# Ten value slots and a new order of the loads in a decoder step with cached attention

## The chip, the core and the metric

The kernel runs on one core of a Trainium2 chip. The metric is the device time of one execution in microseconds (us), of which the median of several executions counts.

## The reference, cut to what matters

One layer of a decoder works on 512 prompt tokens and on 8 sample sequences of 8 new tokens each (64 tokens). All of it is 32-bit floating point.

```
proj = x @ w_in                       # (576 tokens, 1024) @ (1024, 4096)
q, k, v, g_att, b, c, h, g_conv = split(proj, 8)      # 512 wide each
att = dilated_attention(q, [cache_k; k], [cache_v; v]) * silu(g_att)
z   = b * conv3(c * h) * silu(g_conv)
y   = layer_norm(alpha * x + [att, z] @ w_out)
```

Attention has 8 heads of 64. The prompt attends to itself; each sample also attends to a cache of 2,048 past positions, of which the three windows (128 by 1, 512 by 4, 2048 by 16) touch 1,280. The outputs hold y, the new keys and values, the convolution state, and the whole cache copied and moved on by 8 positions.

## The kernel before, in words

**Tiles and rounds.** The input projection is cut into 32 weight tiles of 1024 x 128 (512 KB each). Three come first, then four rounds (i = 0 to 3), one for each pair of heads, with first tile t0 = 3 + 8i. A round projects c (C), h (H), b (B), the convolution's gate (G_CONV), the next round's values (V), the attention's gate, and the next round's q and k; the last round has five tiles. Each product is made in three passes over a high and a low part of both factors (`product`, L993 to L999), in two halves of 288 tokens, into the PSUM banks `pj_a` and `pj_b`. Between the halves TensorE works on the round's attention: scores, transposes and values of the prompt, scores against the cached keys (four pieces, `sample_scores`, L1084), and products with the cached values (ten pieces, `sample_values`, L1125), spread over the round's last three tiles. After the rounds comes the output projection over `wo`, with the layer norm behind it.

**A weight tile's way.** `load_w` (L227, on SyncE's queue) fills one of two slots of `w_raw`; it waits until the low part of the tile two before is made. `split_hi` on ScalarE (L396) rounds it to `w_hi`, waiting for the load and for TensorE to be done with that slot; `split_lo` on VectorE (L678) makes `w_lo`; then `project` (L1001) may run.

**Cached keys and values.** `load_k(i, c)` (L234) fills one of four slots of `k_buf` (1,280 KB), `load_v(i, n)` (L241) one of `V_SLOTS` = 8 slots of `v_buf` (512 KB), piece n of round i in slot (10i + n) mod 8. A load waits until the piece that lay in its slot is used. All loads are issued in program order by SyncE (L249 to L356), a wait holds up all behind it, and they form one DMA queue. The order by hand is in L282 to L303: in steps j = 0 to 4 of round i a weight tile and then a key piece of round i+1 (in round 0 two value pieces too), then two more weight tiles, values 8 and 9 of round i, `save_v` (the prompt's values out), values 0 and 1 of round i+1, a weight tile, values 2 to 7, `save_k`. Then the eight tiles of `wo` (L307) go into the room of `k_buf` and its neighbours, each as its room comes free, and last values 8 and 9 of round 3 (L328).

**Copies of the cache.** 60 DMAs from HBM to HBM copy the cache's parts to the outputs (24 of the unused part, 16 of keys with 1,280 KB, 20 of values; 1,024 KB each but the keys'). ScalarE issues them with `copy_next` (L434) between its other work, on its own queue: 5 before the rounds, 12 in each of rounds 0 to 2, 10 in the last, the rest behind it. The end of the kernel waits for all of them (L358).

**ScalarE and VectorE** each run a list written by hand (`act_round` L556, `act_last_round` L605, `dve_round` L853, `dve_last_round` L894). In the last round the splits of `wo` (`split_wo` L538, `split_wo_lo` L794) lie between the exponentials of the gates (`exp_gate` L502) and the pieces of the gates (`gate_half` L759). `gate_half` makes 1 + exp, its reciprocal, the product with `zb` (the convolution's result, from `conv_out_half` L824) or with `o_pr`, and the product with the bank of the gate's projection (L777), which frees that bank for the next `project`. `out_sample` (L527) copies the sample's attention from the bank `sc` to `o_s`; `sample_out_turn` (L1149) transposes it in the next round. `y_pad` holds the convolution's sums (`conv_taps`, L780).

Of the kernel before, what the change touches and what calls it, by code (L numbers as in the profile page):

```python
# [7 lines left out]
P = 128  # L8
# [36 lines left out]
V_SLOTS = 8  # L45
# [26 lines left out]
def layer_step(nc, d):  # L72

    with ExitStack() as ctx:
# [16 lines left out]
        zb = sb("zb", [P, NT])  # L91
# [26 lines left out]
        o_s = sb("o_s", [P, 2 * P], stack=early)  # L118
# [46 lines left out]
        g_exp, g_step = sem("g_exp"), sem("g_step")  # L165
# [7 lines left out]
        v_stage = gcs  # L173

# [51 lines left out]
        def _(sp):  # L226
# [55 lines left out]
            for i in range(NPAIR - 1):  # L282
                t0 = tile0(i)
                for j in range(5):
                    load_w(t0 + 3 + j)
                    if j:
                        load_k(i + 1, j - 1)
                    if i == 0 and j < 4:
                        load_v(0, 2 * j)
                        load_v(0, 2 * j + 1)  # L290
                load_w(t0 + 8)
                load_w(t0 + 9)
                load_v(i, 8)
                load_v(i, 9)
                save_v(i + 1)
                load_v(i + 1, 0)
                load_v(i + 1, 1)
                load_w(t0 + 10)
                for n in range(2, 8):
                    load_v(i + 1, n)  # L300
                save_k(i + 1)
            load_w(W_TILES - 2)
            load_w(W_TILES - 1)  # L303

# [8 lines left out]
            load_wo(0)  # L313
            sp.wait_ge(k_used, pieces + 2)
            load_wo(1)
            sp.wait_ge(k_used, pieces + 3)
            load_wo(2)
            sp.wait_ge(k_used, pieces + 4)
# [9 lines left out]
            load_v(NPAIR - 1, 8)  # L328
            load_v(NPAIR - 1, 9)
# [65 lines left out]
        def _(act):  # L395
# [86 lines left out]
            copy_next()  # L482
# [73 lines left out]
            def act_round(i):  # L556
# [10 lines left out]
                copy_next()  # L567
# [37 lines left out]
            def act_last_round(i):  # L605
# [23 lines left out]
                split_wo(1)  # L629
                out_prompt(i)  # L630
# [8 lines left out]
                split_wo(4)  # L639
                split_wo(5)  # L640
# [9 lines left out]
                copy_next()  # L650
                for t in TOKEN_TILES[1:]:
                    if t == QT:
                        out_sample_turned(i)
                        split_sample()
                    else:
# [21 lines left out]
        def _(dve):  # L677
# [81 lines left out]
            def gate_half(i, gate, h):  # L759
# [9 lines left out]
                if gate == 0:  # L769
                    nc.vector.tensor_tensor(rg[:, c], rg[:, c], zb[:, c], ALU.mult).then_inc(g_step, 1)  # L770
# [9 lines left out]
            def conv_taps(i, tap):  # L780
                n = PAD_COLS - 2
                cw = conv_w[:, i * CONV_WIDTH + tap:i * CONV_WIDTH + tap + 1]
                if tap == 0:
# [3 lines left out]
                    dve.wait_ge(padded, i + 1)  # L787
                    nc.vector.tensor_scalar(y_pad[:, 0:n], u_pad[:, 0:n], cw, None, ALU.mult).then_inc(y_step, 1)
# [625 lines left out]
```

## Time and profile before

| | us |
|---|---|
| median of 3 executions | 382.79 (381.42 to 383.18) |
| the profiled execution, its own time | 379.59 |
| its span, first to last instruction | 377.5 |
| TensorE busy (PE) | 353.8 |
| VectorE, ScalarE busy | 198.5, 117.4 |
| DMA moved | 141.06 MB, mean 374 GB/s |

The profile is of one execution. PE is TensorE's matmuls, PEld its weight loads, DVE is VectorE, ACT ScalarE, POOL GpSimd; SPq and ACTq are the issues of DMAs by SyncE and ScalarE. Times are us from the first instruction. A wait is named by the instruction that waited and by what ended its wait. Matmul records count from issue to their modelled end, so a busy PE says that it is fed, not that it is at its peak.

### The profile page before, as it was taken

To read this page: it belongs to the slowest core of one execution; us is meant where nothing else is said; L and a number is where in the kernel's file an instruction comes from. 1 tells how busy PE (TensorE), PEld (TensorE's weight loads), DVE (VectorE), ACT (ScalarE), POOL (GpSimd) and SP (SyncE) were. 2 spreads that over 40 slices of the span, in tenths; PEclk is the share of its full clock that TensorE was granted. 3 is DMA by queue.
4 is the path that set the end of the run, shared out by engine and by line. 5 is a ranking of instruction groups with operands and counts; after the bars stand their busy time and mean duration, and the time that the engine had idled before them with its cause. 6 is when DMAs were issued, how large, how long until landed. Compare 5 with 4: busy or idle time off the path is not lost.

```text
span 377.5 us, 7664 instructions
## 1 busy us (share of the span) xinstructions
PE 353.8 (94%) x3256; PEld 311.3 (82%) x3256; DVE 198.5 (53%) x371; ACT 117.4 (31%) x236; POOL 10.9 (3%) x28
## 2 busy tenths in 40 slices
PE   1999999997999999999999799999998998999991
PEld 1899888896988888999988689999787997888780
DVE  2533446817314368571242486711536799284765
ACT  4523423313213243431241243412525643220100
POOL 0010000000000000001000000010000002000000
PEclk9999999998999999999999999999999999999997
DMA  7999999999999999899999999999999886999931
GB/s 279 408 413 423 419 417 423 419 423 422 413 416 418 421 379 413 316 403 369 394 418 418 383 418 395 423 394 406 415 416 408 326 333 216 366 317 366 361 124 56
DMA packets 34547, 141.06 MB, mean 374 GB/s; under 512 B 3409, under 2 KB 3793, under 8 KB 32465
## 3 DMA queue, kind: packets, MB, share of 16 engines
q1 hardware_dynamic: 18194, 73.46, 48.9%
q10 hardware_dynamic: 16320, 67.11, 45.8%
q8 instruction: 26, 0.43, 0.4%
q14 instruction: 7, 0.06, 0.0%
HBM read 135.80 MB, written 71.86 MB: 550 GB/s over the span
## 4 chain that ended last, share of the span: by engine, by line
PE 62%; DMA 28%; DVE 4%; ACT 2%; SPq 2%; issue 1%; ACTq 0%
DMA w_raw<-in_w_tiles 26%; PE pj_a L997 7%; PE pj_b L997 6%; PE pj_a L999 6%; PE pj_a L998 6%; PE pj_b L998 6%; PE pj_b L999 6%; PE sc L1136 5%; PE px L1294 3%; PE px L1296 3%; PE px L1295 3%; PE sc L1100 2%; DVE w_lo L681 2%; ACT w_hi L402 2%; DMA k_buf<-in_xT 2%; PE po L1079 1%
## 5 line engine op out<-in xcount | busy, mean ns | idle before, releaser
L997 PE MATMUL pj_a<-x_hi,w_hi 128*128 128x288 f32 x256 | 79.8, 312 | 9.7 <-DVE x_lo L688 8.3
L997 PE MATMUL pj_b<-x_hi,w_hi 128*128 128x288 f32 x256 | 79.1, 309 | 0.0
L998 PE MATMUL pj_a<-x_lo,w_hi 128*128 128x288 f32 x256 | 76.5, 299 | 0.0
L999 PE MATMUL pj_a<-x_hi,w_lo 128*128 128x288 f32 x256 | 76.5, 299 | 0.0
L998 PE MATMUL pj_b<-x_lo,w_hi 128*128 128x288 f32 x256 | 76.1, 297 | 0.0
L999 PE MATMUL pj_b<-x_hi,w_lo 128*128 128x288 f32 x256 | 75.9, 297 | 0.0
L681 DVE TENSOR_TENSOR w_lo<-w_raw,w_hi 128x1024 fp32r<-128x1024 f32 x32 | 39.1, 1223 | 50.9 <-ACT w_hi L402 50.9
L997 PEld LDWEIGHTS pj_a<-x_hi,w_hi 128*128 128x128 f32 x256 | 49.2, 192 | 18.3 <-issue 9.3
L402 ACT CAST w_hi<-w_raw 128x1024 fp32r<-128x1024 f32 x32 | 33.5, 1046 | 87.3 <-DMA w_raw<-in_w_tiles 55.6
L997 PEld LDWEIGHTS pj_b<-x_hi,w_hi 128*128 128x128 f32 x256 | 48.6, 190 | 4.1 <-issue 2.6
L998 PEld LDWEIGHTS pj_a<-x_lo,w_hi 128*128 128x128 f32 x256 | 49.3, 193 | 0.0
L999 PEld LDWEIGHTS pj_a<-x_hi,w_lo 128*128 128x128 f32 x256 | 49.2, 192 | 0.0
L998 PEld LDWEIGHTS pj_b<-x_lo,w_hi 128*128 128x128 f32 x256 | 48.6, 190 | 0.0
L999 PEld LDWEIGHTS pj_b<-x_hi,w_lo 128*128 128x128 f32 x256 | 48.5, 190 | 0.0
L767 DVE RECIPROCAL rg<-rg 128x288 f32<-128x288 f32 x16 | 31.2, 1953 | 0.6
L488 ACT ACTIVATE p_pr<-p_pr,stat 128x512 f32<-128x512 f32 (+3 forms) x32 | 17.7, 555 | 27.1 <-DVE stat L732 27.1
L732 DVE CUSTOM_DVE_ANT_0 p_pr<-px,mask_pr 128x512 f32<-128x512 f32 (+3 forms) x32 | 14.4, 486 | 18.8 <-PE px L1049 18.8
L1136 PE MATMUL sc<-v_buf,pt_s 128*32 128x128 f32 x640 | 21.4, 276 | 0.0
L1100 PE MATMUL sc<-k_buf,q_bd 128*32 128x320 f32 x256 | 20.5, 438 | 0.9 <-DVE stat L754 0.9
L1294 PE MATMUL px<-wo,x_hi 128*128 128x512 f32 x48 | 19.1, 397 | 1.2 <-issue 1.2
L1296 PE MATMUL px<-wo,x_lo 128*128 128x512 f32 x48 | 19.0, 396 | 0.0
L1136 PEld LDWEIGHTS sc<-v_buf,pt_s 128*32 128x32 f32 x640 | 16.3, 109 | 3.3 <-issue 3.0
(124 smaller groups left out, 403.4 us busy)
## 6 DMA issues: line engine op xcount, KB each, us to landing
k_buf<-in_k_used SPq DMA_DIRECT2D x16, 1280.0 KB, 15.2
v_buf<-in_v_used SPq DMA_DIRECT2D x40, 512.0 KB, 18.4
out_k_used_out<-in_k_used ACTq DMA_DIRECT2D x16, 1280.0 KB, 11.6
out_v_used_out<-in_v_used ACTq DMA_DIRECT2D x20, 1024.0 KB, 10.8
w_raw<-in_w_tiles SPq DMA_DIRECT2D x32, 512.0 KB, 11.5
out_k_rest_out<-in_k_rest ACTq DMA_DIRECT2D x12, 1024.0 KB, 11.5
out_v_rest_out<-in_v_rest ACTq DMA_DIRECT2D x12, 1024.0 KB, 11.3
wo_raw<-in_w_out SPq DMA_DIRECT2D x8, 512.0 KB, 8.6
```

Of the source, the lines that this page charges most:

```text
L402: nc.scalar.copy(w_hi[:, c], w_raw[:, c]).then_inc(w_hi_done, 1)
L488: nc.scalar.activation(p, p, ACT.Exp, bias=negmax_pr[:, e:e + 1], scale=-1.0, accum_out=sum_pr[:, e:e + 1]).then_inc(pr_exp, 1)
L681: nc.vector.tensor_tensor(w_lo[:, c], w_raw[:, c], w_hi[:, c].bitcast(F32), ALU.subtract)\
L732: nc.vector.tensor_tensor_reduce(out=p_pr[:, e * SEQ:e * SEQ + w], in0=px[e][:, 0:w], in1=mask_pr[:, SEQ - w:], scale=-SCALE, scalar=BIG, ...
L767: nc.vector.reciprocal(rg[:, c], rg[:, c]).then_inc(g_step, 1)
L997: nc.tensor.matmul(out, w_hi[:, w], x_hi[:, c], start=(k == 0), stop=False)
L998: nc.tensor.matmul(out, w_hi[:, w], x_lo[:, c], start=False, stop=False)
L999: return nc.tensor.matmul(out, w_lo[:, w], x_hi[:, c], start=False, stop=(k == KT - 1))
L1100: last = nc.tensor.matmul(sc[r * 32:r * 32 + 32, 0:K_COLS], q, k_buf[:, k0:k0 + K_COLS], start=(b == 0), stop=(b == 1 and not ends), skip_ ...
L1136: last = nc.tensor.matmul(sc[r * 32:r * 32 + 32, b * P:(b + 1) * P], pt_s[:, t * P + r * 32:t * P + r * 32 + 32], v_buf[:, v0:v0 + P], sta ...
L1294: nc.tensor.matmul(out, x_hi[:, tok], wo[:, hi], start=(n == 0), stop=False)
L1296: last = nc.tensor.matmul(out, x_lo[:, tok], wo[:, hi], start=False, stop=(n == KT - 1))
```

## The change

Four things. `v_buf` has ten slots instead of eight, one for each piece of a round. Room for them comes from two buffers that go: z is written over the convolution's sums in `y_pad` instead of to `zb`, and the sample's attention `o_s` lies in the first 256 columns of `y_pad`. The gate's product with z is for the second half two instructions (224 and 64 columns) instead of one, and the first convolution tap waits in rounds 1 to 3 for the transposes of `o_s`. SyncE's order is new: each of the steps j = 0 to 4 loads a weight tile and then values 2j and 2j+1 of the same round, keys of the next round follow (three at the round's end, the fourth in the next step 0), and in the last round the values are loaded between the last weight tiles and the first tiles of `wo`. Four of ScalarE's cache copies go later: one from before the rounds and one from each of rounds 0 to 2; two of them are issued in the last round, one at its end and one in the output projection.

```diff
--- before.py
+++ after.py
@@ -42,7 +42,7 @@
 K_COLS = USED // K_PIECES
 K_SLOT = DEC_BATCH * K_COLS
 V_PIECES = 10
-V_SLOTS = 8
+V_SLOTS = V_PIECES
 QT = SEQ // P
 X_CHUNKS = ((0, 1), (1, 3), (3, 5), (5, 7), (7, 8))
 PAD_COLS = 2 + SEQ + DEC_BATCH * (2 + DEC_SEQ)
@@ -88,7 +88,6 @@
         w_lo = sb("w_lo", [P, 2 * 1024], F32R)
         mix = sb("mix", [P, 2 * NHP * NT])
         gcs = sb("gcs", [P, NT])
-        zb = sb("zb", [P, NT])
         rg = sb("rg", [P, NT])
         u_pad = sb("u_pad", [P, PAD_COLS])
         y_pad = sb("y_pad", [P, PAD_COLS])
@@ -115,7 +114,6 @@
         v_new = sb("v_new", [NS, 2 * P], stack=early)
         pt_s = sb("pt_s", [P, (USED_TILES + 1) * P], stack=early)
         v_buf = sb("v_buf", [P, V_SLOTS * 1024], stack=early)
-        o_s = sb("o_s", [P, 2 * P], stack=early)
         o_pr = sb("o_pr", [P, SEQ], stack=early)
         early.close()
         as_loaded = ctx.enter_context(ExitStack())
@@ -162,7 +160,7 @@
             sem("s_masked"), sem("s_max"), sem("s_exp"), sem("s_inv"), sem("s_norm"))
         s_turned, s_moved, s_pv, s_out = sem("s_turned"), sem("s_moved"), sem("s_pv"), sem("s_out")
         so_turned, so_moved, s_mixed = sem("so_turned"), sem("so_moved"), sem("s_mixed")
-        g_exp, g_step = sem("g_exp"), sem("g_step")
+        g_exp, g_step, g_prompt = sem("g_exp"), sem("g_step"), sem("g_prompt")
         m_hi_done, m_lo_done, wo_hi_done, wo_lo_done = (
             sem("m_hi_done"), sem("m_lo_done"), sem("wo_hi_done"), sem("wo_lo_done"))
         low_read, r_high = sem("low_read"), sem("r_high")
@@ -171,6 +169,8 @@
 
         x_raw = k_buf[:, 0:KT * NT]
         v_stage = gcs
+
+        o_s = y_pad[:, 0:2 * P]
 
 
         xs = w_hi[:, 0:KT * P].rearrange("p (k two t) -> p k two t", two=2, t=NS)
@@ -280,27 +280,30 @@
             load_k(0, 3)
             save_k(0)
             for i in range(NPAIR - 1):
+
+
                 t0 = tile0(i)
                 for j in range(5):
                     load_w(t0 + 3 + j)
-                    if j:
-                        load_k(i + 1, j - 1)
-                    if i == 0 and j < 4:
-                        load_v(0, 2 * j)
-                        load_v(0, 2 * j + 1)
+                    if i and j == 0:
+                        load_k(i, 3)
+                    load_v(i, 2 * j)
+                    load_v(i, 2 * j + 1)
                 load_w(t0 + 8)
+                load_k(i + 1, 0)
                 load_w(t0 + 9)
-                load_v(i, 8)
-                load_v(i, 9)
                 save_v(i + 1)
-                load_v(i + 1, 0)
-                load_v(i + 1, 1)
+                load_k(i + 1, 1)
                 load_w(t0 + 10)
-                for n in range(2, 8):
-                    load_v(i + 1, n)
+                load_k(i + 1, 2)
                 save_k(i + 1)
             load_w(W_TILES - 2)
+            load_k(NPAIR - 1, 3)
+            load_v(NPAIR - 1, 0)
+            load_v(NPAIR - 1, 1)
             load_w(W_TILES - 1)
+            load_v(NPAIR - 1, 2)
+            load_v(NPAIR - 1, 3)
 
 
 
@@ -311,10 +314,16 @@
             pieces = K_PIECES * (NPAIR - 1)
             sp.wait_ge(k_used, pieces + 1)
             load_wo(0)
+            load_v(NPAIR - 1, 4)
+            load_v(NPAIR - 1, 5)
             sp.wait_ge(k_used, pieces + 2)
             load_wo(1)
+            load_v(NPAIR - 1, 6)
+            load_v(NPAIR - 1, 7)
             sp.wait_ge(k_used, pieces + 3)
             load_wo(2)
+            load_v(NPAIR - 1, 8)
+            load_v(NPAIR - 1, 9)
             sp.wait_ge(k_used, pieces + 4)
             load_wo(3)
             load_wo(4)
@@ -325,8 +334,6 @@
             load_wo(6)
             sp.wait_ge(s_masked, K_PIECES * NPAIR)
             load_wo(7)
-            load_v(NPAIR - 1, 8)
-            load_v(NPAIR - 1, 9)
 
 
             sp.wait_ge(s_pv, NPAIR)
@@ -479,7 +486,6 @@
             copy_next()
             copy_kk(0)
             split_hi(4)
-            copy_next()
 
             def exp_prompt(i, u):
                 for e in range(2):
@@ -564,7 +570,6 @@
                 split_hi(t0 + 2)
                 copy_next()
                 move_prompt(i, 0)
-                copy_next()
                 exp_prompt(i, 1)
                 split_hi(t0 + 3)
                 move_prompt(i, 1)
@@ -627,6 +632,7 @@
                 split_hi(t0 + 4)
                 copy_next()
                 split_wo(1)
+                copy_next()
                 out_prompt(i)
                 move_sample(i, 0)
                 move_sample(i, 1)
@@ -637,6 +643,7 @@
                 split_wo(3)
                 exp_gate(t0 + G_CONV, 1)
                 split_wo(4)
+                copy_next()
                 split_wo(5)
                 exp_gate(gate_tile(i), 0)
                 copy_next()
@@ -648,10 +655,12 @@
                 out_sample(i)
                 copy_next()
                 copy_next()
+                copy_next()
                 for t in TOKEN_TILES[1:]:
                     if t == QT:
                         out_sample_turned(i)
                         split_sample()
+                        copy_next()
                     else:
                         split_mix(1 + t)
                         copy_next()
@@ -766,8 +775,14 @@
                 dve.wait_ge(g_step, step + 1)
                 nc.vector.reciprocal(rg[:, c], rg[:, c]).then_inc(g_step, 1)
                 dve.wait_ge(g_step, step + 2)
-                if gate == 0:
-                    nc.vector.tensor_tensor(rg[:, c], rg[:, c], zb[:, c], ALU.mult).then_inc(g_step, 1)
+                if gate == 0 and h == 0:
+                    nc.vector.tensor_tensor(rg[:, c], rg[:, c], y_pad[:, c], ALU.mult).then_inc(g_step, 1)
+                elif gate == 0:
+                    nc.vector.tensor_tensor(rg[:, HALF:SEQ], rg[:, HALF:SEQ], y_pad[:, HALF:SEQ], ALU.mult)\
+                        .then_inc(g_prompt, 1)
+                    r = rg[:, SEQ:].rearrange("p (b t) -> p b t", t=DEC_SEQ)
+                    nc.vector.tensor_tensor(r, r, y_s[:, :, 0:DEC_SEQ], ALU.mult).then_inc(g_step, 1)
+                    dve.wait_ge(g_prompt, i + 1)
                 else:
                     dve.wait_ge(pr_out, i + 1)
                     e = slice(h * HALF, min((h + 1) * HALF, SEQ))
@@ -785,6 +800,9 @@
                     dve.wait_ge(pj_read[0], tile0(i) + 2)
                     dve.wait_ge(pj_read[1], tile0(i) + 2)
                     dve.wait_ge(padded, i + 1)
+                    if i:
+
+                        dve.wait_ge(so_turned, i)
                     nc.vector.tensor_scalar(y_pad[:, 0:n], u_pad[:, 0:n], cw, None, ALU.mult).then_inc(y_step, 1)
                 else:
                     dve.wait_ge(y_step, 2 * i + tap)
@@ -826,12 +844,12 @@
                 dve.wait_ge(y_done, i + 1)
                 dve.wait_ge(pj_done[h], tile0(i) + B + 1)
                 if h == 0:
-                    nc.vector.tensor_tensor(zb[:, 0:HALF], pj[0][:, 0:HALF], y_pad[:, 0:HALF], ALU.mult)\
+                    nc.vector.tensor_tensor(y_pad[:, 0:HALF], pj[0][:, 0:HALF], y_pad[:, 0:HALF], ALU.mult)\
                         .then_inc(pj_read[0], 1)
                 else:
-                    nc.vector.tensor_tensor(zb[:, HALF:SEQ], pj[1][:, 0:HP_LEFT], y_pad[:, HALF:SEQ], ALU.mult)\
+                    nc.vector.tensor_tensor(y_pad[:, HALF:SEQ], pj[1][:, 0:HP_LEFT], y_pad[:, HALF:SEQ], ALU.mult)\
                         .then_inc(z_done, 1)
-                    nc.vector.tensor_tensor(zb[:, SEQ:].rearrange("p (b t) -> p b t", t=DEC_SEQ),
+                    nc.vector.tensor_tensor(y_s[:, :, 0:DEC_SEQ],
                                             pj[1][:, HP_LEFT:HALF].rearrange("p (b t) -> p b t", t=DEC_SEQ),
                                             y_s[:, :, 0:DEC_SEQ], ALU.mult).then_inc(pj_read[1], 1)
```

## Rows read from the trace of the kernel before

**Rows 1.** The page: PE's busy time, TensorE's clock and DMA in 40 slices of 9.4 us.
```profile
PE 353.8 (94%) x3256; PEld 311.3 (82%) x3256; DVE 198.5 (53%) x371; ACT 117.4 (31%) x236; POOL 10.9 (3%) x28
...
PEclk9999999998999999999999999999999999999997
DMA  7999999999999999899999999999999886999931
```
**Rows 2.** Waits of PE, whole span: line waited for: us in total, times, longest.
```profile
PE pj_a L997 <- DVE x_lo L688: 8.3, 2, 7.2
PE po L1079 <- ACT pt_pr L494: 3.0, 3, 1.3
PE pj_a L997 <- DVE mix L777: 1.2, 1, 1.2
PE px L1294 <- issue: 1.2, 1, 1.2
PE sc L1100 <- DVE stat L754: 0.9, 1, 0.9
PE pt L1120 <- ACT pt_s L515: 0.9, 1, 0.9
```
**Rows 3.** Chain of waits, 83 to 92 us: start us, us, what.
```profile
63.14 20.74 DMA w_raw<-in_w_tiles
...
89.55 0.58 PE pj_a L997
```
**Rows 4.** Busy by stretch: PE, PEld, DVE, ACT, POOL, clock, DMA share, GB/s.
```profile
89.00:92.00 3.00, 2.45 (x10) 2.48 (x11) 2.93 (x5) 0.00 (x0) 0.00 (x0) 0.56 1.02 425
92.00:96.00 4.00, 4.00 (x53) 3.64 (x52) 1.91 (x3) 1.77 (x4) 0.00 (x0) 0.91 1.01 419
```
**Rows 5.** Timeline, 208 to 216 us.
```profile
210.99 1.05 ACT L402 CAST w_hi<-w_raw 128x1024 fp32r<-128x1024 f32 x1 [11.18 <-DMA w_raw<-in_w_tiles]
...
212.84 0.88 PE L1079 MATMUL po<-pt_pr,v_rows 128*64 128x128 f32 x12 [1.31 <-ACT pt_pr L494]
...
214.59 1.28 PE L1100 MATMUL sc<-k_buf,q_bd 128*32 128x320 f32 x16 [0.87 <-DVE stat L754]
```
**Rows 6.** Timeline of SyncE's issues, 245 to 302 us.
```profile
245.86 2.12 SPq L246 DMA_DIRECT2D v_buf<-in_v_used  x2
```
**Rows 7.** Landing of the two v_buf loads issued in 246 to 248 us.
```profile
DMA to landing us min/median/max: 9.0/10.3/11.6
```
**Rows 8.** Timeline of PE, 257.5 to 259.5 us.
```profile
258.44 1.08 PE L1136 MATMUL sc<-v_buf,pt_s 128*32 128x128 f32 x32
```
**Rows 9.** Landing of the weight tile issued in 245 to 246 us.
```profile
DMA to landing us min/median/max: 6.4/6.4/6.4
```
**Rows 10.** DMA by queue, 252 to 262 us (q1 SyncE's, q10 ScalarE's): packets, MB, share.
```profile
q1 hardware_dynamic: 590, 1.61, 41.4%
```
**Rows 11.** DMA by queue, 262 to 290 us.
```profile
q1 hardware_dynamic: 1994, 7.01, 61.8%
q10 hardware_dynamic: 1180, 4.54, 40.2%
```
**Rows 12.** Timeline of ScalarE, 255 to 330 us.
```profile
298.43 1.07 ACT L540 CAST wo<-wo_raw 128x1024 fp32r<-128x1024 f32 x1
...
300.55 1.05 ACT L540 CAST wo<-wo_raw 128x1024 fp32r<-128x1024 f32 x1
```
**Rows 13.** Timeline of VectorE, 300 to 309 us.
```profile
303.00 0.46 DVE L770 TENSOR_TENSOR rg<-rg,zb 128x288 f32<-128x288 f32 x1
303.49 0.46 DVE L777 TENSOR_TENSOR mix<-pj_a,rg 128x288 f32<-128x288 f32 x1
```
**Rows 14.** Chain of waits, 296 to 322 us.
```profile
305.30 0.33 PE pj_a L997
...
309.67 0.33 PE pj_b L997
```
**Rows 15.** DMA issues, 316 to 362 us.
```profile
out_v_used_out<-in_v_used ACTq DMA_DIRECT2D x11, 1024.0 KB, 16.8
```

## The prediction

> **What bounds the kernel now.** The page first: PE is busy 353.8 us of 377.5, and the slices show it fed from the second to the last; the DMA engines are just as full until about 290 us [rows 1]. So two resources lie close together, and the waits must say which one decides. PE's waits name 15.5 us in all. Of these 8.3 us are the start (x must land) and 1.2 us the step to the output projection; what is left inside is 6.0 us in a few places [rows 2]. TensorE therefore sets the time, and the loads set it only where they are late enough to stop it.
>
> Two places are made by late loads. The first is at 86 to 89.5 us. The chain shows a weight tile issued at 63.14 that landed after 20.74 us; behind it ScalarE and VectorE, which work in a fixed order, did the gate late, and PE began its next tile at 89.55 [rows 3]. PE lost 0.85 us (L1120) and 1.23 us (L777), rounded in the view [rows 2]. Right after it the granted clock of 89 to 92 us is 0.56 of full speed and of 92 to 96 us 0.91 [rows 4]: TensorE fell from 2.4 to 1.2 GHz for a time, which cost 3 x 0.44 + 4 x 0.09 = 1.7 us more. The second is at 211: ScalarE waited 11.18 us for a weight tile until 210.99, and PE lost 1.31 and 0.87 us [rows 5]. Both times the tile stood in SyncE's queue behind key and value pieces.
>
> One edge costs nothing in this profile, but is thin. Value piece 9 of round 2 is the second of two issued from 245.86 on (so at about 246.5), and takes 11.6 us [rows 6, 7]: it lands at 258.1. PE starts on pieces 8 and 9 at 258.44, 1.08 us for both [rows 8], so it needs piece 9 at 258.9: 0.8 us to spare. The edge is in every one of rounds 0 to 2, since the piece waits for a slot. The profiled execution took 379.59 us and the median 382.79, 3.2 us more; this edge is where I would look for them, but no row shows it.
>
> **The change, part by part.** *Ten slots and the new order, rounds 0 to 2.* Before, a round's last eight value loads came as a burst at its end, with one weight tile behind six of them, and in steps 1 to 3 of round 0 each carried a weight tile, a key piece and two value pieces (0.52 + 1.31 + 1.05 = 2.9 MB). Now a step is a tile and two values, 1.6 MB, and the keys come behind. The tile that took 20.74 us loses two key pieces ahead of it, 2.6 MB, and one copy beside it. At SyncE's rate of 7.01 MB in 28 us, 0.25 MB/us [rows 11], that is 10 us earlier, and 2.1 us would give PE its wait back. The tile of 211 had the round's ten value issues (5.2 MB) put ahead of it from 169 us on, now two key pieces (2.6 MB): again 2.6 MB or 10 us, where 2.2 us are enough. I take both stalls and the slow clock as gone: 0.85 + 1.23 + 1.7 + 1.31 + 0.87 = 6.0 us gained. Bounds: 2.2 us (only one goes) to 7 us (the 0.67 and 1.05 us at L1079 in the last round shrink too; they come from the order of ScalarE's list, so I expect them to stay). No wait on a slot is new: a value piece now waits for the same piece of the round before, which is long used. Keys are issued 25 us and more ahead of use.
>
> *Values 8 and 9* now come with step 4, some 25 us before use, so the thin edge goes. I count half of the 3.2 us, 1.6 us, for the median and nothing for the profiled execution; bounds 0 and 3.2.
>
> *The last round pays.* Ten values and a key piece are now loaded there, where two values were. Count what SyncE's queue must move after 252 us, when the weight tile issued at 245.49 has landed in 6.4 us, so the queue is nearly empty [rows 9]. Until `wo` tile 2 these are, in order: outputs 0.30, key 1.31, tile 0.52, key 1.31, output 0.30, tile 0.52, key 1.31, values 0 and 1 1.05, tile 0.52, values 2 and 3 1.05, wo0 0.52, values 4 and 5 1.05, wo1 0.52, values 6 and 7 1.05, wo2 0.52: 11.9 MB. Before, the queue moved 1.61 MB from 252 to 262 and 7.01 MB from 262 to 290 [rows 10, 11], 8.6 MB by 290. So wo2 lacks 3.2 MB, at 0.25 MB/us 13.0 us: it lands at 303.0. ScalarE took it at 298.43 [rows 12]: `split_wo(2)` stands 4.6 us longer, and behind it on ScalarE the gate's exponential. The chain from there ended with the gate's product at 303.49 + 0.46 = 303.95, which frees the bank; PE began that tile only at 305.30 [rows 13, 14], so 1.35 us are covered, and 3.2 us reach PE. wo3 lies 1.57 MB behind, 309.3 instead of the 300.55 of its split [rows 12]. Its two splits take 1.05 and 1.2 us, the next gate half 3.3 us (the chain of rows 13 once more), to 314.9; PE comes there at 309.67 + 3.2 = 312.9 [rows 14]: 2.0 us more. Debt 5.2 us. Wo4 to wo7 (2.1 MB, 8.4 us, to 317.7) are needed for the output projection, which would start at 322: covered.
>
> The rate is the unknown. At the full 0.41 MB/us of both queues together [rows 11] wo2 lands at 298 and the debt is 0. At the 0.16 MB/us of 252 to 262 [rows 10] it lands at 310 and the debt passes 10 us. I take 0.25, since ScalarE's copies there are issued as in 262 to 290. Two things I set off against each other: four copies there are of 1,280 KB instead of 1,024 (+1.05 MB), and one copy less waits in the queue at 252.
>
> *Copies.* Before 252 us four are gone, a relief for the rounds that is in the gain already. Eleven were issued after 316 us [rows 15], now 13, 2.1 MB more. The DMA slices fall to 3 and 1 tenths only in the last 19 us [rows 1], and 2.1 MB at the page's 374 GB/s is 5.6 us: hidden. Cover gone, it would be those 5.6 us.
>
> *z in `y_pad`, `o_s` in `y_pad`.* One product of 0.46 us [rows 13] becomes two, at most 0.46 us more in each of four rounds, hidden by the 1.35 us above and by VectorE's own waits. The new wait of the first tap is for transposes that PE does two tiles earlier; VectorE's list stands behind it, but it ends before. Nothing.
>
> **Sum.** -6.0 + 5.2 = -0.8 us for the profiled execution, 378.8; for the median 382.8 - 0.8 - 1.6 = 380.4 us.
>
> **The rivals.** *No debt (B).* ScalarE's copies are issued from its list, so once it stands at a split no copy follows and SyncE's queue gets nearly everything. For it: at 290 to 310 the DMA slices were below full [rows 1]. Then 382.8 - 6.0 - 1.6 = 375.2 us. Against it: two or three copies are already queued when the wait begins.
>
> *A larger debt (C), the slower side.* While both queues have work they share evenly, 0.205 MB/us each (half of 0.41). wo2 then lands at 290 + 3.24/0.205 = 305.8, 6.1 us reach PE; wo3 at 313.5, its gate half ends at 319.1, PE comes at 315.7: 3.4 us more. Debt 9.5 us, 382.8 - 6.0 + 9.5 = 386.3 us (the saved edge comes back as another one in the last round). It decides from 0.22 MB/us down. For it: in 252 to 262 SyncE's queue had only 1.61 MB in 10 us [rows 10]. Against it: 7.01 to 4.54 MB in the 28 us behind [rows 11]. The Trainium skill (DMA: Bandwidth & Descriptors, Queues, rings and completion order) says that each DMA engine takes turns between the queue rows for which it has work; by that rule C holds wherever a copy is pending, and the 7.01 to 4.54 would only mean that at times none was.
>
> *It does not do what it says (D).* The median's waits come from something else than the loads, and gain and debt cancel: 382.8 us.
>
> **How the numbers follow.** A measurement of this kernel tells a change from none from about 0.5% on, 1.9 us: faster is below 380.9, slower above 384.7. The forecast case (debt 3.5 to 6.5 us, 378.7 to 381.7) has 0.41, of which 0.27 faster and 0.14 same. B 0.16, all faster. C 0.27, all slower. D 0.16: 0.01 faster, 0.11 same, 0.04 slower. Together faster 0.44, same 0.25, slower 0.31. The range takes in B's edge and C: 375.0 to 387.0. The likeliest case's own range is 378.7 to 381.7 us.
>
> **What would show it.** Right: no wait of PE of over 0.5 us between 80 and 230 us, no fall of the clock there, weight tiles landing in 6 to 14 us, value 9 tens of us before use; then ScalarE waiting at L540 for wo2 and wo3, and PE waiting before the two halves of the last gate's tile. B would show those splits without a wait. C would show 6 us before the first half. The forecast is wrong if PE waits for keys in rounds 1 to 3, if the last copy lands after the last y, or if the early waits stay where they are though the loads land early.

## The result, and the profile after

The change makes the kernel slower by 1%: 387.06 us median of 13 executions (384.54 to 390.07) against 383.18 us (380.18 to 384.91), ratio 1.0102 with a 95% interval of 1.0075 to 1.0129. The forecast was 380.4 us, faster; the range ended at 387.0, and the rival with the larger debt stood at 386.3. A single profiled execution can lie off its median: the one of before took 379.59 us, 3.6 us below its median, the one after 385.67 us, 1.4 us below. So differences between the two traces overstate the loss of the medians (3.9 us) by some 2 us.

The page of the profile after, the lines that answer to [rows 1], and PE's waits over the whole span, which answer to [rows 2]:

```profile
PE 356.8 (93%) x3256; PEld 314.2 (82%) x3256; DVE 200.0 (52%) x375; ACT 118.0 (31%) x236; POOL 11.9 (3%) x28
...
PEclk9999999999999999999999999999996969999998
DMA  7999999599999995999999989999999996999991
```
```profile
PE pj_a L1015 <- DVE x_lo L697: 8.5, 2, 7.4
PE po L1097 <- ACT pt_pr L500: 6.9, 3, 5.3
PE pj_a L1015 <- DVE mix L792: 2.6, 1, 2.6
PE px L1312 <- issue: 0.8, 1, 0.8
PE pj_a L1015 <- ACT gcs L459: 0.2, 1, 0.2
```

The DMA slices now have three dips before 235 us (the two 5s and the 8): the rounds have DMA time to spare. PE has no wait between the start (the first 20 us) and 265 us; the two early stalls and the slow clock there are gone. The gain shows at the first tile of the last round. The timeline of PE has it in the kernel before, and then in the one after, at:

```profile
260.02 0.40 PE L997 MATMUL pj_a<-x_hi,w_hi 128*128 128x288 f32 x1
```
```profile
254.41 0.40 PE L1015 MATMUL pj_a<-x_hi,w_hi 128*128 128x288 f32 x1
```

That is 5.6 us earlier, where 6.0 were forecast. From there on it is lost and more. ScalarE's timeline after, at the splits of the `wo` tiles (start, duration, and in brackets what it waited for), answers to [rows 12]:

```profile
291.72 1.04 ACT L546 CAST wo<-wo_raw 128x1024 fp32r<-128x1024 f32 x1 [10.67 <-DMA wo_raw<-in_w_out]
292.67 1.41 ACT L515 ACTIVATE p_s<-p_s,stat 128x1344 f32<-128x1344 f32 x1
...
294.08 0.41 ACT L500 COPY pt_pr<-pt 128x128 f32<-128x128 f32 x2
...
303.76 1.05 ACT L546 CAST wo<-wo_raw 128x1024 fp32r<-128x1024 f32 x1 [5.16 <-DMA wo_raw<-in_w_out]
...
309.10 1.05 ACT L546 CAST wo<-wo_raw 128x1024 fp32r<-128x1024 f32 x1 [3.57 <-DMA wo_raw<-in_w_out]
```

And PE's timeline, the two waits that follow from these:

```profile
294.54 0.69 PE L1097 MATMUL po<-pt_pr,v_rows 128*64 128x128 f32 x4 [5.33 <-ACT pt_pr L500]
```
```profile
309.41 0.58 PE L1015 MATMUL pj_a<-x_hi,w_hi 128*128 128x288 f32 x1 [2.60 <-DVE mix L792]
```

Read them as one chain. ScalarE stood at `split_wo(0)` for 10.67 us until wo0 landed; the sample's exponential and the move of the prompt's last probabilities (L500) are behind it in its list; PE waited 5.33 us for that move. The same tile that PE began at 305.30 before [rows 14] begins at 309.41. PE's last matmul, in the kernel before and in the one after:

```profile
369.02 0.40 PE L1296 MATMUL px<-wo,x_lo 128*128 128x512 f32 x1
```
```profile
375.46 0.40 PE L1314 MATMUL px<-wo,x_lo 128*128 128x512 f32 x1
```

It ends at 375.9 instead of 369.4. From the first tile of the last round to that end it was 109.4 us and is 121.5: a debt of 12 us between these two traces, against 5.2 forecast. 7.4 us are more waiting (10.3 us instead of 2.9 from 262 us on), and most of the rest is the slow clock around the waits, in the busy time by stretch (the last three numbers are the clock as a share of 2.4 GHz, the DMA share and GB/s):

```profile
289.00:295.00 6.00, 0.67 (x6) 0.29 (x4) 1.98 (x3) 3.28 (x6) 0.00 (x0) 0.72 1.03 421
295.00:300.00 5.00, 4.85 (x30) 4.62 (x27) 4.22 (x7) 2.94 (x5) 0.00 (x0) 0.65 1.02 419
307.00:316.00 9.00, 6.59 (x44) 6.35 (x48) 7.84 (x11) 3.86 (x5) 0.00 (x0) 0.62 1.00 394
```

The last views are the two queues, the one of 262 to 290 us answering to [rows 11] (q1 SyncE's, q10 ScalarE's: packets, MB, share):

```profile
q1 hardware_dynamic: 1431, 5.89, 51.3%
q10 hardware_dynamic: 1284, 5.77, 50.0%
```

SyncE's queue moved 5.89 MB instead of 7.01. These were the theories when the experiments began: V, what SyncE's queue has to bring in the last round fixes when the `wo` tiles land; with the rivals O (their place behind the values), C (the copies moved there), K (the clock) and L (the in-order lists, which pass a wait for `wo` on to TensorE).

### The profile page after: what moved, and what is told of

It is laid out like the page before. It is cut to its first block, busy times and chain, and to the rows that moved or that the text cites. A ratio compares the mean times of both kernels' runs of the same rounds, so it can differ in the third digit from the quotient of the medians.

```text
span 383.9 us, 7672 instructions
## 1 busy us (share of the span) xinstructions
PE 356.8 (93%) x3256; PEld 314.2 (82%) x3256; DVE 200.0 (52%) x375; ACT 118.0 (31%) x236; POOL 11.9 (3%) x28
## 4 chain that ended last, share of the span: by engine, by line
PE 83%; DMA 8%; SPq 3%; DVE 3%; ACT 1%; issue 1%; ACTq 0%; DVEq 0%
PE pj_a L1015 10%; PE pj_b L1015 9%; PE pj_a L1016 8%; PE pj_a L1017 8%; PE pj_b L1017 8%; PE pj_b L1016 8%; DMA wo_raw<-in_w_out 6%; PE sc L1154 5%; PE sc L1118 4%; PE px L1312 3%; PE px L1314 3%; PE px L1313 3%; PE px L1067 3%; PE po L1097 2%; SPq L246 2%; PE pt L1084 2%
## 5 line engine op out<-in xcount | busy, mean ns | idle before, releaser
L1015 PE MATMUL pj_a<-x_hi,w_hi 128*128 128x288 f32 x256 | 80.9, 316 | 11.3 <-DVE x_lo L697 8.5
L1016 PE MATMUL pj_a<-x_lo,w_hi 128*128 128x288 f32 x256 | 77.4, 302 | 0.0
L1017 PE MATMUL pj_a<-x_hi,w_lo 128*128 128x288 f32 x256 | 77.3, 302 | 0.0
L1015 PEld LDWEIGHTS pj_a<-x_hi,w_hi 128*128 128x128 f32 x256 | 50.1, 196 | 19.9 <-issue 10.7
L1016 PEld LDWEIGHTS pj_a<-x_lo,w_hi 128*128 128x128 f32 x256 | 50.2, 196 | 0.0
L1017 PEld LDWEIGHTS pj_a<-x_hi,w_lo 128*128 128x128 f32 x256 | 50.1, 196 | 0.0
L500 ACT COPY pt_pr<-pt 128x512 f32<-128x512 f32 (+3 forms) x32 | 12.0, 429 | 28.0 <-PE pt L1084 28.0
## 6 DMA issues: line engine op xcount, KB each, us to landing
out_k_rest_out<-in_k_rest ACTq DMA_DIRECT2D x12, 1024.0 KB, 10.7
```

The source lines that it names most:

```text
L500: nc.scalar.copy(pt_pr[:, e * SEQ:e * SEQ + width(u)], pt[e][:, 0:width(u)]).then_inc(pr_moved, 1)
L1015: nc.tensor.matmul(out, w_hi[:, w], x_hi[:, c], start=(k == 0), stop=False)
L1016: nc.tensor.matmul(out, w_hi[:, w], x_lo[:, c], start=False, stop=False)
L1017: return nc.tensor.matmul(out, w_lo[:, w], x_hi[:, c], start=False, stop=(k == KT - 1))
```

## The experiments

All ratios are to the kernel before, run on the same chip; that kernel's median was 380.9 to 381.0 us in them. "Last matmul" and landings are of the one profiled execution of each.

### Fewer bytes in the last round

```diff
# SyncE, on the changed kernel (cut)
                     load_w(t0 + 3 + j)
+                    if i == 2 and 1 <= j <= 3:
+                        load_k(3, j - 1)
...
+                load_k(3, 3)                       # round 2, with tile t0 + 8
+                for n in range(4): load_v(3, n)    # behind tile t0 + 10
```


> The changed kernel, but in round 2 the keys of round 3 are loaded as before the change (one piece in each of steps 1 to 3, the fourth behind), and values 0 to 3 of round 3 come behind the last weight tiles of round 2: 3.9 MB of keys and 1.0 MB of values leave the last round's queue. Theory V (volume: what SyncE's queue must bring in the last round fixes when the wo tiles land, and the early gain is lost against it): wo0 lands before 284 us instead of 291.7, wo2 before 295 instead of 303.7, the PE waits of 5.3 and 2.6 us go below 1 us each, both slow-clock stretches of the last round go; the last matmul 10 to 12 us earlier, ratio to the kernel before 0.975 to 0.985. Rival O (order: it is only that values stand ahead of wo): less than 3 us better, ratio 1.00 to 1.01. Rival C (the two copies moved into the last round): unchanged, 1.01.

Measured: 380.54 us, ratio 1.0007 (0.9981 to 1.0032). wo0 was split at 286.3 and wo2 at 295.7 us, 5.5 and 8.0 us earlier. ScalarE's wait for wo0 shrank from 10.7 to 3.7 us and no longer reached PE, but then ScalarE waited 6.3 us for wo3:

```profile
295.73 1.05 ACT L548 CAST wo<-wo_raw 128x1024 fp32r<-128x1024 f32 x1 [1.44 <-DMA wo_raw<-in_w_out]
303.79 1.05 ACT L548 CAST wo<-wo_raw 128x1024 fp32r<-128x1024 f32 x1 [6.29 <-DMA wo_raw<-in_w_out]
```

PE's 5.3 us wait became one of 3.7 at the gate's second half. The last matmul ended 5.1 us earlier, where theory V said 10 to 12, and the ratio fell by 1.0%, where it said 2.5 to 3.5%: V has the direction and a third to a half of the size. The ratio lies in the range of rival O as well, so this run does not decide between them; the next one does.

### The wo tiles ahead of the values

```diff
# SyncE, last round, in short
             load_wo(1)
-            (values 2 to 9 spread before and between wo0 to wo2)
+            load_v(3, 2); load_v(3, 3)
             load_wo(2); load_wo(3)
+            for n in range(4, 10): load_v(3, n)
             load_wo(4)
```


> The changed kernel, but in the last round the wo tiles 0 to 3 are issued ahead of values 2 to 9 as far as they may be (values 2 and 3 behind wo1, values 4 to 9 behind wo3, then wo4 to wo7). Same bytes. Theory V: wo0 lands 1.05 MB, 5 us, earlier, so the first PE wait falls from 5.3 to about 0.5 us; but all else is still late, wo4 to wo7 and values 4 to 9 land near 305 to 317 us, so PE waits move behind it: 2 to 4 us better than the change, ratio 1.000 to 1.005. Rival O: all waits of the last round go, ratio 0.98 to 0.985. Rival C: as the change, 1.01.

Measured: 388.32 us, ratio 1.0214 (1.0180 to 1.0248). The worst of all, and none of the theories said so. Up to its end no wait of PE in the last round is longer than 0.9 us, nearly as said; but wo4 now stood behind six values, and ScalarE's list has the last gate's exponentials and the split of z behind it:

```profile
311.66 1.04 ACT L542 CAST wo<-wo_raw 128x1024 fp32r<-128x1024 f32 x1 [13.07 <-DMA wo_raw<-in_w_out]
```
```profile
312.00:323.00 11.00, 0.00 (x0) 0.00 (x0) 10.11 (x9) 6.17 (x10) 3.40 (x2) 0.65 1.00 384
323.00:330.00 7.00, 6.59 (x18) 5.21 (x18) 6.29 (x8) 1.67 (x2) 0.00 (x0) 0.57 1.02 310
```

From 312 to 323 us PE did nothing, and then began the output projection at half speed: one wait of 11.7 us. So rival O falls. With the same bytes, this order only moved the wait, to the end of the round, where nothing covers it. wo7 came to its split at 315.4 us, in the changed kernel at 317.1.

### The copies back in their old places

```diff
# ScalarE: one copy_next() again before the rounds and one in each of rounds 0 to 2;
# the ones behind split_wo(1), split_wo(4), out_sample and split_sample removed
```


> The changed kernel with ScalarE's four cache copies back in their old places (two fewer issued in the last round, four more before). Theory V: wo0 and the wait of 5.3 us stay (both copies are issued behind wo1 and wo4); wo3 and behind 1 to 2.5 us earlier; ratio 1.003 to 1.010. Rival C: both waits go, ratio 0.98 to 0.985.

Measured: 380.69 us, ratio 1.0010 (0.9981 to 1.0038): the whole 1%, a little more than theory V allowed, and not by way of C, since PE still waits 3.5 us for the gate and 2.5 us at the output projection. wo0 landed 4.8 us earlier (286.9), against the expectation, though the two copies that the change had added to the last round stand behind it in ScalarE's list. The queues of 262 to 290 us say why:

```profile
q1 hardware_dynamic: 1702, 6.86, 59.8%
q10 hardware_dynamic: 1237, 4.79, 41.9%
```

SyncE's queue has 0.97 MB more. The copies come in a fixed sequence, 24 of 1,024 KB, then 16 keys of 1,280 KB, then 20 of 1,024: with four fewer issued before, the four around the last round's start are keys, 1.05 MB more in ScalarE's queue.

### The size of those copies

```diff
# same number of copies at the same places; the 16 key copies first, then the other 24
+ n = (n + 24) % 40   for the first 40
```


> The changed kernel with the sequence of the cache copies changed: the 16 key copies of 1,280 KB first, then the 24 of the unused part, so that those issued from 244 to 268 us have 1,024 KB. Same number of copies at the same places. Theory Z (the 1.05 MB more in ScalarE's queue around the last round, which the prediction set off against a shorter queue, delay the wo tiles): wo0 lands 3 to 5 us earlier (287 to 289 us), SyncE's queue moves 6.5 MB or more from 262 to 290 us instead of 5.9, ratio 1.000 to 1.006. Rival N (only the number of copies in the last round counts): wo0 as in the change, ratio 1.01.

Measured: 381.75 us, ratio 0.9995 (0.9953 to 1.0038), with a wide scatter (377.3 to 383.9). The profiled execution was one of the longer ones (383.36), so its waits and its last matmul are not compared here. wo0 was split at 283.5, 8.3 us earlier, where 3 to 5 were expected. The queues:

```profile
q1 hardware_dynamic: 1723, 7.03, 61.2%
q10 hardware_dynamic: 1192, 4.62, 40.5%
```

7.03 MB, the 7.01 of [rows 11] again. Theory Z holds: the order of the sizes alone, with all counts and places kept, undoes the loss. The key copies now run in the early rounds, and the last round still began at 255.1 us, so they cost little there.

### No copies in the last round

```diff
# the 10 copies that ScalarE issues in act_last_round up to split_mix(1) are not issued
- copy_next()
+ next(copies)
```
This kernel leaves ten pieces of the cache out of its outputs; it only shows what the queue does without them.

> The changed kernel without the 10 cache copies that ScalarE issues up to the end of the last round (they are left out of the output; its own 12 less the 2 behind). Theory S (SyncE's queue is held back by the copies that share the 16 DMA engines with it): the queue moves near 0.4 MB/us when no copy is pending, wo0 lands before 282 us instead of 291.7, wo7 before 300, both long waits of PE go, the last matmul near 363 us: ratio 0.965 to 0.980. Rival Q (the queue of SyncE has a limit of its own of 0.21 to 0.25 MB/us): wo0 still lands at 286 to 291 and waits of 2 us or more stay, ratio 0.995 or more.

Measured: 373.45 us, ratio 0.9775 (0.9730 to 0.9820).

```profile
q1 hardware_dynamic: 2736, 10.60, 93.8%
q10 hardware_dynamic: 56, 0.21, 1.9%
```

Without copies beside it SyncE's queue moved 10.60 MB in 28 us, 0.38 MB/us, and wo0 and wo7 landed at 278.7 and 295.7. No wait of PE in the last round is longer than 1.3 us, and the last matmul ends at 363.3. Theory S holds and Q falls: the queue has no limit of its own near 0.25; what it gets is what ScalarE's copies leave.

### Copies behind the last round instead

```diff
# ScalarE, last round (cut)
                 split_wo(1)
-                copy_next()
 ...             split_wo(4)
-                copy_next()
 ...             out_sample(i)
+                copy_next(); copy_next()
```


> The changed kernel with the two copies that were moved into the last round issued after it instead; the early four stay away. Theory T (total bytes on the 16 DMA engines up to the last wo tile count, whoever issues them): the wo tiles land at least as early as with the copies in their old places, wo7 by 311 us, PE waits of the last round 5 us in all instead of 10, last copy lands at about the end of the kernel; ratio 0.998 to 1.003. Rival (only copies before the last round matter, because they fill idle DMA time): no better than the change, 1.01; the tail may even be held up by the last copy.

Measured: 384.33 us, ratio 1.0085 (1.0056 to 1.0114). wo0 stays late (290.1, since the four keys stay where they were) and PE waits 3.9 us for it; wo7 landed at 312.7 and the last copy at 376.5 us of a span of 380.5. The two moved copies are worth little in the median: the rival's 1.01 lies in the interval, theory T's 0.998 to 1.003 does not. The profiled execution was the fastest of the twelve (382.30), so its times flatter this kernel, and whether the last copy ends some of its executions stays open.

### The clock held up

```diff
+def fill(count):    # into bank px[1], idle there; results unused
+    for _ in range(count): matmul(px[1], x_hi[:, 0:128], x_hi[:, 0:512])
...
+                fill(22)
                 prompt_values(i, 3)
...
+                fill(10)
                 project(gate_tile(i), 0)
```


> The changed kernel with 22 and 10 extra matmuls (128 x 512, into a bank that is idle there, results unused) just before the two long waits of PE in the last round, 4.7 and 2.1 us of work inside waits of 5.3 and 2.6 us. Theory K (half of the loss is TensorE's clock falling after the two waits): the waits end when they did, but the granted clock stays at 2.4 GHz, the two stretches of 6.8 us at half speed go; the last matmul 3 to 6 us earlier, ratio to the kernel before 0.995 to 1.003. Rival V alone (the landings of the wo tiles set the end, the clock is hidden in the waits): no gain or 1 us worse, 1.010 to 1.014.

Measured: 386.93 us, ratio 1.0146 (1.0096 to 1.0196). The two long waits are filled (one of 1.7 and one of 0.9 us are left at the gate) and the clock stays up to 312 us and beyond:

```profile
289.00:300.00 11.00, 11.00 (x90) 9.48 (x92) 6.30 (x9) 6.23 (x10) 0.00 (x0) 1.00 1.03 420
300.00:312.00 12.00, 10.29 (x106) 8.98 (x97) 6.50 (x8) 3.79 (x7) 0.00 (x0) 1.00 1.03 419
```

and nothing is gained. The first output matmul stands at 322.77 us, in the changed kernel at 323.17:

```profile
315.98 1.05 ACT L546 CAST wo<-wo_raw 128x1024 fp32r<-128x1024 f32 x1 [0.45 <-DMA wo_raw<-in_w_out]
```
```profile
322.77 0.74 PE L1319 MATMUL px<-wo,x_hi 128*128 128x512 f32 x1 [2.47 <-issue]
```

Theory K falls, and the reason is not the last `wo` tile: its split on ScalarE is over at 317.0 us, 5.7 us before that matmul. What comes just before is VectorE's list. VectorE's timeline in the changed kernel, and its waits from 309.5 to 323 us there and in this run:

```profile
320.12 2.35 DVE L815 TENSOR_TENSOR wo<-wo_raw,wo 128x1024 fp32r<-128x1024 f32 x2
322.38 1.28 DVE L821 TENSOR_TENSOR x_lo<-mix,x_hi 128x512 fp32r<-128x512 f32 x2
```
```profile
DVE wo L815 <- ACT wo L546: 0.9, 1, 0.9
```
```profile
DVE wo L815 <- ACT wo L546: 0.8, 1, 0.8
```

In both, VectorE waits once, for the split of wo3, and then works without a wait through two gate halves and the low parts of wo3 to wo7 up to the low part of x (L821) that the output projection needs. wo3 was split at 309.10 us in the changed kernel and at 308.70 here, 0.4 us earlier, and so is the first output matmul. TensorE at half speed only used time that it would have spent waiting for VectorE. Behind that matmul the clock is at 0.77 from 323 to 330 us (1.00 in the changed kernel), so the fall came later instead.

### The splits behind the work that TensorE waits for

```diff
# ScalarE, last round
-split_wo(0); exp_sample; move_prompt(3); split_hi(t0+4); split_wo(1); out_prompt; move_sample(0), (1)
-split_wo(2); exp_gate(G_CONV, 0); move_sample(2); split_wo(3); exp_gate(G_CONV, 1); split_wo(4), (5)
-exp_gate(gate, 0); split_wo(6), (7); exp_gate(gate, 1); split_mix(0), (1)
+exp_sample; move_prompt(3); split_hi(t0+4); out_prompt; move_sample(0), (1); exp_gate(G_CONV, 0)
+split_wo(0); move_sample(2); exp_gate(G_CONV, 1); split_wo(1); exp_gate(gate, 0); split_wo(2)
+exp_gate(gate, 1); split_mix(0); split_wo(3); split_mix(1); split_wo(4) to (7)
# VectorE likewise: split_wo_lo(0) behind the first gate half, (3) to (7) around split_mix_lo
```


> The changed kernel with ScalarE's and VectorE's lists of the last round reordered: the splits of the wo tiles stand behind the work that TensorE waits for (exponentials, moves, gate halves), and wo3 to wo7 come last. Loads as in the change. Theory L (a late wo tile costs only because the in-order lists pass its wait on to TensorE; it is needed only in the output projection): no wait over 1 us in the last round, no fall of the clock, the 5.6 us gained before are kept; last matmul near 366 us instead of 375.9, ratio 0.980 to 0.990. Rival V (the wo tiles' landing sets the end anyway): the wait moves in front of the output projection, last matmul 370 to 374, ratio 0.997 to 1.007.

Measured: 379.79 us, ratio 0.9974 (0.9944 to 1.0003). The long waits for the gate and for the move are gone, but the tiles land later still: wo7 at 320.4. ScalarE, no longer held up, issues its copies earlier, and its queue moved 4.12 MB from 290 to 310 us, where it was 3.11. PE then waited for value 9 and in the output projection for the splits:

```profile
PE sc L1154 <- DMA v_buf<-in_v_used: 1.9, 1, 1.9
PE px L1312 <- DVE wo L815: 1.9, 3, 1.1
```

The last matmul ends at 369.0, between L and V, but the ratio is V's (0.997 to 1.007), not L's (0.980 to 0.990). Taken with the copies' runs: the lists are the way by which late loads reach TensorE, the queue is the reason why they are late.

```diff
# both of the edits above, on the changed kernel
+copy_next()    before the rounds, and in each of rounds 0 to 2
-copy_next()    behind split_wo(1), split_wo(4), out_sample, split_sample
```


> The same reordered lists, with the four copies in their old places. Theory L: wo7 lands some 4 us earlier than in splits_late, the start of the output projection too; 0.980 to 0.988. Rival V: 0.990 to 0.998, since the wo tiles land by 311 us.

Both together: 372.96 us (372.72 to 373.70), ratio 0.9793 (0.9757 to 0.9829), faster than either kernel. All waits of PE:

```profile
PE pj_a L1013 <- DVE x_lo L695: 9.1, 2, 7.2
PE po L1095 <- ACT pt_pr L501: 1.5, 2, 0.9
PE pt L1310 <- DVE x_lo L819: 0.4, 1, 0.4
PE pj_a L1013 <- ACT gcs L459: 0.2, 1, 0.2
```

The last matmul ends at 363.0 us, 6.5 before that of the kernel before: the early gain is kept. Against copies_back (1.0010), which has the same loads and copies, the order of the lists is worth 2.2%.

### The reordered lists and the ten slots by themselves

```diff
# on the kernel before, in short: the same order of ScalarE's and VectorE's last-round lists
-split_wo(0)
 exp_sample ... exp_gate(G_CONV, 0)
+split_wo(0)
...
```


> The kernel before (eight slots, old orders of loads and copies) with the last round's lists of ScalarE and VectorE reordered as in splits_late. Theory L (the reordering only keeps what the new load order gains): 0.996 to 1.001. Rival (the reordering alone makes the gain of splits_late_copies_back): 0.985 or less.

The kernel before with the reordered lists: 380.44 us, ratio 0.9963 (0.9930 to 0.9997). A little, a fifth of the 2.1%, so the lists alone do not make the gain of the last version. That it needs the whole new load order is not shown: the reordered lists were not run with the kernel that follows here. Its profile caught the thin edge at work, PE waiting 1.8 us for value 9 of round 0:

```profile
109.14 0.65 PE L1136 MATMUL sc<-v_buf,pt_s 128*32 128x128 f32 x16 [1.76 <-DMA v_buf<-in_v_used]
```

```diff
# on the kernel before, with the new buffers (cut)
+V_SLOTS = V_PIECES
...
-load_w(t0 + 8); load_w(t0 + 9)
 load_v(i, 8); load_v(i, 9)
+load_w(t0 + 8); load_w(t0 + 9)
...
 load_w(W_TILES - 1)
+load_v(NPAIR - 1, 8); load_v(NPAIR - 1, 9)
...
 load_wo(7)
-load_v(NPAIR - 1, 8); load_v(NPAIR - 1, 9)
```


> The kernel before with ten value slots and the new buffers, the old orders of loads and copies, but values 8 and 9 of a round issued with the tile of step 4 instead of two tiles later. If the thin edge at value 9 costs the median execution (the 1.6 us of the prediction): ratio 0.993 to 0.998, and value 9 lands 15 us before its use. If not: 0.998 to 1.002. The early waits at 88 and 211 us stay in both.

Measured: 377.42 us (376.51 to 379.12), ratio 0.9884 (0.9844 to 0.9924), better than either forecast of it. Value 9 of rounds 1 and 2 landed some 10 us before its use, and of the waits of [rows 5] nothing is left, since the two pieces no longer stand ahead of the later tiles; the two waits near 88 us stay:

```profile
PE pt L1129 <- ACT pt_s L515: 1.3, 1, 1.3
PE pj_a L1006 <- DVE mix L783: 1.2, 1, 1.2
```

But the clock did not fall behind them. The stretch of 89 to 92 us, which has the clock at 0.56 in [rows 4], is here:

```profile
89.00:92.00 3.00, 1.91 (x14) 1.94 (x15) 2.93 (x5) 0.00 (x0) 0.00 (x0) 1.00 1.02 425
```

It is at 1.00 in the traces of before_splits_late and alias_only too, which have the old load order as well.

```diff
# on the kernel before: z over y, o_s in y_pad; V_SLOTS, load order and copies as before
-zb = sb("zb", [P, NT])
-o_s = sb("o_s", [P, 2 * P], stack=early)
+o_s = y_pad[:, 0:2 * P]
...
+g_prompt, and VectorE's wait for so_turned
```


> The kernel before with only the new buffers: z over y_pad, o_s in y_pad, the split gate product and the tap's new wait; eight value slots, the old order of loads and copies. All theories: nothing, ratio 0.998 to 1.002. A rival A (the sharing of y_pad costs time by a new wait) would give 1.005 or more.

The new buffers alone: 380.42 us, ratio 0.9997 (0.9970 to 1.0024). They cost nothing that can be seen, and rival A falls. Here too the profile shows one wait of 1.9 us for value 9 of round 0 (L1145, the only wait of PE on a DMA).

## Why the prediction was wrong

*The early gain* was right for the profiled execution: 5.6 us against 6.0, both stalls and the slow clock gone, no new wait on keys. But the 1.7 us of slow clock in the sum were seen in that one execution only: three other traces have the old load order (one with values 8 and 9 moved) and no slow clock at 89 us. The two with the order unchanged have a wait for value 9 in its place, and begin the last round at 259.7 and 261.3 us, so the size came out by luck in part.

*The thin edge* was real. The profile of before hides it; two other executions with the same load order show waits of 1.8 and 1.9 us there, in round 0. Moving just that load (with ten slots) gives 1.2%, or 4.4 us, of which 2.2 us are the waits at 211 us. Some 2.2 us are left for the edge and all else that moved, against 1.6 forecast; the two were not measured apart.

*The new buffers* cost nothing, as said.

*The step that failed is "two things I set off against each other"*: the 1.05 MB of larger copies against one copy less in the queue. The shorter queue did not show; the larger copies did. From 262 to 290 us SyncE's queue moved 5.89 MB where 7.01 were assumed, 0.21 MB/us instead of 0.25. (From 252 to 262 us it moved 2.36 MB, not 1.61, so the two stretches together fall short by only 0.4 MB; but all was due 5.6 us earlier.) The sum's times are those of the kernel before, so it should be read with TensorE's gain taken off: wo0 at 290.4 - 5.6 = 284.8 us. It landed at 291.7, 7 us later. 3.9 us of these arose before its count began, since the weight tile issued at 239.88 took 10.3 us to land instead of 6.4; the rest because the 8.7 MB behind it took 41.5 us instead of 38.4. With the small copies in place (small_copies_last) the same two took 7.1 and 35.8 us, and the time came back.

*Rival C* stood at 0.205 MB/us, debt 9.5 and 386.3 us, slower by 0.9%; measured 1.0%. Its even split is there in the 5.89 to 5.77 MB, but its time is right in part by luck: it looked for 6 us of waiting before the gate's first half, where 2.6 us are, and the longest wait stands at a place that it did not cost. The Trainium skill (DMA: Bandwidth & Descriptors, Queues, rings and completion order) says that each DMA engine takes turns between the queue rows for which it has work. The traces agree: in 262 to 290 us of the kernel before SyncE's queue got 60% of the bytes, but there ScalarE's queue at times moved next to nothing, as from 264 to 267 us:

```profile
q1 hardware_dynamic: 336, 1.22, 101.0%
q10 hardware_dynamic: 10, 0.02, 1.7%
```

*Rival B's* way is seen too, behind the longest wait: ScalarE had stood at its split and issued nothing, and from 292 to 296 us of the changed kernel SyncE's queue had nearly all.

```profile
q1 hardware_dynamic: 420, 1.53, 93.6%
q10 hardware_dynamic: 49, 0.14, 8.4%
```

*wo0 and wo1 were left out.* The sum began at wo2. It put the path from wo0 at nothing without a reason, though wo0 was split at 286.84 before, the moment when it landed, and by the sum's own bytes it would land at 290.4, 3.6 us later on the same clock. The longest wait, 5.33 us, is there. wo2 and wo3 were forecast for 303.0 and 309.3 us and landed at 303.7 and 309.1, and that looks better than it is: on the sum's clock, where PE is 5.6 us later, they landed at 309.3 and 314.7, 6.3 and 5.4 us late.

*The clock* fell in both waits (most of the 4.7 us of the last round's 12 that are not waits), which the sum had not; but holding it up gave nothing, so here it is no term of its own: wo3's landing and VectorE's list behind it set the start of the output projection.

*That the copies go late is a relief* was the wrong way round. Before 252 us there is DMA time to spare now, and with the four copies back there the last round still began at 253.8 us; the last round has none. The prediction did not compare the two stretches' bytes as a whole, though the numbers were in it.

## What to carry to other kernels

When loads are moved from a stretch into a later one, add up the bytes of all queues in both stretches, background copies with their sizes too: a queue gets what the others leave, here 0.38, 0.25 or 0.21 MB/us in the same 28 us. Where an engine runs a list in fixed order, put work on data that is needed late (here the `wo` splits) behind the work that the critical engine waits for; then a late load costs nothing until it is needed. Before a slow clock or a late load is given a price, look which chain ends last there: here it was VectorE's list. And compare the profiled execution with the median and with other traces: a load that lands 0.8 us before its use in one was 1.8 us late in others, and a fall of the clock seen in one was missing in three.

## What was not expected of the hardware

In the changed kernel a wait of PE of 5.3 us and one of 2.6 us each brought 6.8 us at 1.2 GHz by the granted clock, which began within the wait (near 291.6 and 308.7 us). In wo_first a wait of 11.7 us brought 13.7 us of it, while in copies_back waits of 3.5 and 2.5 us left the clock at 2.4 GHz. And two waits near 88 us, 0.9 and 1.2 us, brought a slow stretch in the trace of before, where waits of 1.3 and 1.2 us at the same place in ten_slots_old_order brought none. So the price of a wait cannot be read from its length alone, nor from one execution.

What one queue gets hangs on what the other has pending: 1.0 MB more in ScalarE's queue (5.77 MB against 4.79 in copies_back) took 1.0 MB from SyncE's in 28 us. The uneven splits of the other kernels come at least in part from stretches in which ScalarE's queue moved next to nothing (0.02 MB from 264 to 267 us before).
